# Summing modulation products over partitions: a transposing pass on VectorE and four matmuls per group of blocks, in place of four matmuls per block

## The reference, cut to what matters

```
def modulation(cond, w, b):
    m = jax.nn.silu(cond) @ w + b            # cond 1 x 1024, w 1024 x 9216, per layer and condition
    return m.reshape(cond.shape[0], 1, N_MOD, D_MODEL)
...
hp = hp + 0.5 * adaln_gate(m_ctx, 0) * swiglu(adaln_input(hp, m_ctx, 0, norm_g[i, 0]), ...)
hs = hs + 0.5 * adaln_gate(m_lat, 0) * swiglu(adaln_input(hs, m_lat, 0, norm_g[i, 0]), ...)
```

## Time and profile before

| | |
|---|---|
| device time, median of 3 runs | 1719.74 us (1719.39 to 1721.28) |
| profiled execution: span from first to last instruction | 1717.1 us |
| what lies around the span (median less span) | 2.6 us |
| TensorE busy | 1660.1 us, 97% of the span |
| VectorE busy | 1067.5 us, 62% |
| ScalarE busy | 578.3 us, 34% |
| mean granted TensorE clock | 0.976 of full speed |

### The profile page before, as it was taken

The page is one execution under the profiler, slowest core; times in us unless marked ns, Lnnn a source line. Parts: engine busy times, 40 slices in busy tenths (PEclk is TensorE's granted clock), DMA queues, the critical chain, the costliest instruction groups (busy, mean ns, idle before and its releaser), DMA issues.

```text
span 1717.1 us, 25878 instructions
## 1 busy us (share of the span) xinstructions
PE 1660.1 (97%) x9927; PEld 1589.1 (93%) x9927; DVE 1067.5 (62%) x1803; ACT 578.3 (34%) x751; POOL 81.3 (5%) x48
## 2 busy tenths in 40 slices
PE   8899999988899899999989999998999998999998
PEld 4899999988756899999989999998999998999998
DVE  3677668767754766767966777697745435334323
ACT  2423232253344442322234333222642325333222
POOL 1200000034100100000010000001000001000000
PEclk9999999989999899999989999999999998999999
DMA  9755547526200445555634545564533332433332
GB/s 310 187 182 164 192 159 244 170 85 207 77 1 31 157 146 173 177 189 196 224 120 135 193 161 195 190 226 157 186 124 96 125 123 85 136 122 122 124 130 77
DMA packets 222917, 261.81 MB, mean 152 GB/s; under 512 B 14502, under 2 KB 207494, under 8 KB 222854
## 3 DMA queue, kind: packets, MB, share of 16 engines
q1 hardware_dynamic: 222854, 260.95, 46.3%
HBM read 258.64 MB, written 2.29 MB: 152 GB/s over the span
## 4 chain that ended last, share of the span: by engine, by line
PE 86%; issue 6%; DVE 4%; ACT 1%; POOL 1%; DMA 0%; POOLq 0%; SPq 0%; ACTq 0%; DVEq 0%
PE ps L1066 15%; PE ps L1067 15%; PE ps L1069 15%; PE ps L1022 9%; PE ps L1024 9%; PE ps L1023 9%; PE ps L1055 3%; PE ps L1037 2%; PE ps L1257 1%; DVE macc L754 1%; PE ps L1126 1%; PE ps L1294 1%; POOL hrs L503 1%; PE ps L1363 1%; DVE w_lo L731 1%
## 5 line engine op out<-in xcount | busy, mean ns | idle before, releaser
L731 DVE TENSOR_TENSOR w_lo<-raw,w_hi 128x2048 fp32r<-128x2048 f32 x164 | 380.0, 2317 | 282.3 <-ACT w_hi L527 282.2
L1066 PE MATMUL ps<-x_hi,w_hi 128*128 128x384 f32 x1536 | 523.3, 341 | 13.2 <-ACT x_hi L553 9.9
L1067 PE MATMUL ps<-x_hi,w_lo 128*128 128x384 f32 x1536 | 520.1, 339 | 0.0
L1069 PE MATMUL ps<-x_lo,w_hi 128*128 128x384 f32 x1536 | 517.1, 338 | 0.0
L527 ACT ACTIVATE w_hi<-raw 128x2048 fp32r<-128x2048 f32 x169 | 322.9, 1911 | 344.2 <-PE ps L1024 326.3
L754 DVE SCALAR_TENSOR_TENSOR macc<-mraw,cT,macc 128x256 f32<-128x256 f32 x896 | 359.9, 478 | 0.0
L1066 PEld LDWEIGHTS ps<-x_hi,w_hi 128*128 128x128 f32 x1536 | 292.1, 190 | 17.0 <-issue 13.3
L1067 PEld LDWEIGHTS ps<-x_hi,w_lo 128*128 128x128 f32 x1536 | 292.1, 190 | 0.0
L1069 PEld LDWEIGHTS ps<-x_lo,w_hi 128*128 128x128 f32 x1536 | 291.3, 190 | 0.0
L1022 PE MATMUL ps<-act_hi,w_hi 128*128 (+1 forms) x832 | 281.8, 339 | 0.0
L1024 PE MATMUL ps<-act_hi,w_lo 128*128 (+1 forms) x832 | 279.6, 336 | 0.0
(11 more groups left out here) (154 smaller groups left out, 1310.7 us busy)
## 6 DMA issues: line engine op xcount, KB each, us to landing
raw<-ffn_w_gu SPq DMA_DIRECT2D x88, 1024.0 KB, 5.1
mraw<-mod_w SPq DMA_DIRECT2D x66, 1024.0 KB, 7.4
raw<-ffn_w_down SPq DMA_DIRECT2D x44, 1024.0 KB, 4.8
raw<-sgu_w_in SPq DMA_DIRECT2D x16, 1024.0 KB, 5.5
raw<-attn_w_in SPq DMA_DIRECT2D x9, 1024.0 KB, 5.0
raw<-sgu_w_out SPq DMA_DIRECT2D x8, 1024.0 KB, 4.8
mfirst<-mod_w SPq DMA_DIRECT2D x6, 1024.0 KB, 12.8
raw<-attn_w_out SPq DMA_DIRECT2D x4, 1024.0 KB, 4.9
```

Source lines behind the costliest of these rows:

```text
L731: nc.vector.tensor_tensor(w_lo[q0 % 2][:, :], raw[q0 % 2][:, :], w_hi[q0 % 2][:, :].bitcast(F32), ALU.subtract).then_inc(lo_done, 1)
L1066: mm(out, hi[:, cols], x_hi[:, k, :], start=(k == 0), stop=False)
L1067: mm(out, lo[:, cols], x_hi[:, k, :], start=False, stop=False)
L1069: last = mm(out, hi[:, cols], x_lo[:, k, :], start=False, stop=(k == KD - 1))
```

## The change

The sum over 128 partitions is split in two. Directly behind each block's `mod_sum`, VectorE runs one `tensor_reduce` with `apply_transpose` over the block's 128 x 512 sums: within each 32 x 32 square it transposes and then adds, so that each group of 32 partitions is summed, and 128 x 16 numbers go to a new tile `red` (room for 18 blocks). It waits for its own engine's last `mod_sum` instruction (`macc_done`). The rest, the sum over the four partition groups, is done by `mod_fold` on TensorE once per group of blocks, with four matmuls (32 columns of weights, `fold`; 4 columns per block moving). There are five groups and the lone first block: 18 blocks (feed-forward 0), 6 (projection and output projection), 18 (feed-forward 1), 18 (feed-forward 2) and 4 (stage V).

`mod_fold` of a group stands in a down stage, behind its last panel but one, and waits for all blocks of the group. `mod_out` is done once per group, behind VectorE's panel steps of that down stage, and TensorE waits for it inside the last panel, before the last bank. The `mod_psum` calls, their waits (`msum_done` in `mod_sum` and in `squares`, `mod_done` in `ffn`, in the attention's transposes and in `ready_ffn`) and the `mod_out` calls beside pairs, after `rotate()` and after the `wsn` products go away. TensorE's loop in `down` is two panels shorter, and these two stand behind it.

```diff
@@ mod_sum
-                if m >= 2:
-                    dve.wait_ge(msum_done, m + ii - 1)
...
                 last.then_inc(macc_done, 1)
+                dve.wait_ge(macc_done, m + ii + 1)
+                nc.vector.tensor_reduce(red[:, bass.ds(b0 - red_base(b0) + ii, 1), :].rearrange("p b n -> p (b n)"),
+                                        acc_of.rearrange("p c (n j) -> p (c n) j", j=32), AX.X, ALU.add,
+                                        apply_transpose=True).then_inc(red_done, 1)
@@ VectorE, ffn pair
-                    if b is not None:
-                        mod_out(b, ii, 1, ps[:, 6 + b % 2, 0:4], (msum_done, b + ii - MOD_SUM + 1))
@@ VectorE, down
                 steps_beside_blocks(dve, 0, blocks, n - 2, step)
+                if group is not None:
+                    mod_out(MOD_GROUPS[group][0], 0, MOD_GROUPS[group][1], ps[:, ORDER[-1], SPARE:SPARE + 4 * MOD_GROUPS[group][1]],
+                            (msum_done, group + 2))
                 gate(idx, j, w)
@@ TensorE
-            def mod_psum(b0, ii, bank, col, alone):
-                pe.wait_ge(macc_done, b0 + ii - MOD_SUM + 1)
-                for a in range(2):
-                    for cond in range(2):
-                        last = mm(ps[:, bank, bass.ds(col + 2 * a + cond, 1)], macc[:, b0 % 2, cond, P * a:P * a + P],
-                                  ones[:, 0:1], start=alone, stop=True, skip_group_check=not alone)
+            def mod_fold(b0, n, bank, col, alone):
+                pe.wait_ge(red_done, b0 + n - MOD_SUM)
+                for q in range(4):
+                    sums = red[:, 0:n, :].rearrange("p b (c a q) -> p b a c q", c=2, a=2)[:, :, :, :, q]
+                    last = mm(ps[32 * q:32 * q + 32, bank, col:col + 4 * n], fold[:, :], sums,
+                              start=alone, stop=True, skip_group_check=not alone)
                 last.then_inc(msum_done, 1)
@@ TensorE, ffn pair
-                    if b is not None:
-                        pe.wait_ge(mod_done, outs_until(b - 1) + ii)
-                        mod_psum(b, ii, 6 + b % 2, 0, True)
@@ TensorE, down
+                        if final and group is not None and m == ORDER[-1]:
+                            pe.wait_ge(mod_done, group + 2)
...
-                        if k == 3 and beside:
-                            mod_psum(block + j0 - 2, 2 * i, ORDER[-1], SPARE + 4 * (j0 - 2) + 8 * i, False)
...
+                    if fold_group is not None:
+                        mod_fold(*MOD_GROUPS[fold_group], ORDER[-1], SPARE, False)
...
-                steps_beside_blocks(pe, 2, min(blocks, n - 3), n - 1, panel)
-                panel(n - 1, 0, beside=blocks == n - 2, final=True)
+                its = (n - 4) // 2
+                if its:
+                    with pe.Fori(0, its) as i:
+                        panel(2, i)
+                        panel(3, i)
+                for j in range(2 + 2 * its, n - 1):
+                    panel(j, 0, fold_group=group if j == n - 2 else None)
+                panel(n - 1, 0, final=True)
@@ TensorE, attention transposes
-                    mod_psum(MOD_M + MOD_IN - 1, 0, 4, 4 * (MOD_IN - 1), True)
-                    pe.wait_ge(mod_done, outs_until(MOD_M + MOD_IN))
```

More of the change, by code:

```diff
@@ L86, in outs_until, with red_base @@
     return n
+def red_base(block):
+    return max([MOD_SUM] + [b for b, n in MOD_GROUPS if b <= block])
 def build(nc, t_in, t_out, toep_dram):
@@ L109, in build @@
             macc = sb("macc", [P, 2, 2, MB], scope=s)
+            red = sb("red", [P, MOD_GU + MOD_DN[0], 16], scope=s)
         sq = sb("sq", [P, 4, T])
@@ L115, in build @@
         mbT = sb("mbT", [P, DEPTH * NMOD * KD])
+        fold = sb("fold", [P, 32])
         ngT = sb("ngT", [P, DEPTH * 3 * KD])
@@ L527, in split, with squares @@
                 nc.scalar.activation(w_hi[q0 % 2][:, :], raw[q0 % 2][:, :], ACT.Copy).then_inc(hi_done, 1)
-            def squares(n, block=0):
+            def squares(n):
                 for k, m in enumerate(ORDER):
                     act.wait_ge(h_done, KD * n + k + 1)
-                    if k == 1 and block:
-                        act.wait_ge(msum_done, block - MOD_SUM)
                     if k >= 4:
@@ L662, in _ @@
             down(Q_OUT0, KD // 2)
-            squares(2, MOD_AT[1])
+            squares(2)
             split(Q_F[1] + 1, 0)
@@ L736, in mod_sum @@
                 m = b0 - MOD_SUM
+                acc_of = macc[:, b0 % 2, :, :]
                 if b0 == MOD_SUM:
@@ L838, in ffn, with down @@
                 loop_pairs(f, dve, pair)
-            def down(q0, n, idx, j, w, block=0, blocks=0):
+            def down(q0, n, idx, j, w, block=0, blocks=0, group=None):
                 def step(j0, i, beside):
@@ L855, in down @@
                         split(q0 + n, 0)
-                    if m == ORDER[-1] and blocks:
-                        mod_out(block, 0, blocks, ps[:, m, SPARE:SPARE + 4 * blocks],
-                                (msum_done, block + blocks - MOD_SUM))
+            dve.wait_ge(const_in, 16)
+            nc.vector.tensor_reduce(fold[:, :], ident[:, :].rearrange("p (g j) -> p j g", j=32), AX.X, ALU.add) \
+                .then_inc(fold_set, 1)
             dve.wait_ge(vecT_pe, 1)
@@ L962, in _ @@
             split(Q_OUT0 + 1, 0)
-            down(Q_OUT0, KD // 2, 1, (0, 1), 1.0, MOD_M + MOD_IN, MOD_OUT)
+            down(Q_OUT0, KD // 2, 1, (0, 1), 1.0, MOD_M + MOD_IN, MOD_OUT, 1)
             vectors(2, (0, 2))
@@ L967, in _ @@
             ffn(1)
-            down(Q_F[1] + 2 * GU, GU, 2, (0, 2), 0.5, MOD_AT[1] + MOD_GU, MOD_DN[1])
+            down(Q_F[1] + 2 * GU, GU, 2, (0, 2), 0.5, MOD_AT[1] + MOD_GU, MOD_DN[1], 2)
             vectors(3, (1, 0))
@@ L1007, in _ @@
                                         act_hi[:, 2 * g:2 * g + 2, :].bitcast(F32), ALU.subtract).then_inc(actl_done, 1)
-            down(Q_OUT1, KS // 2, 4, (1, 1), 1.0)
+            down(Q_OUT1, KS // 2, 4, (1, 1), 1.0, group=4)
             vectors(5, (1, 2))
@@ L1146, in pair, with down, panel @@
                     project(feature_major, q + 2 * g0 + 1, ii, 2)
-                    if b is not None:
-                        pe.wait_ge(mod_done, outs_until(b - 1) + ii)
-                        mod_psum(b, ii, 6 + b % 2, 0, True)
                 loop_pairs(f, pe, pair)
-            def down(q0, n, idx, hi, lo, ready, block=0, blocks=0):
-                def panel(j0, i, beside=False, first=False, final=False):
+            def down(q0, n, idx, hi, lo, ready, group=None):
+                def panel(j0, i, first=False, final=False, fold_group=None):
                     pe.wait_ge(lo_done, q0 + j0 + 2 * i + 1)
@@ L1224, in _ @@
             mod_rows(6)
-            mod_psum(MOD_SUM, 0, 2, 4 * MOD_SUM, True)
+            pe.wait_ge(fold_set, 1)
+            mod_fold(MOD_SUM, 1, 2, 4 * MOD_SUM, True)
             row_transposes(3)
             ffn(0, 0)
-            down(Q_F[0] + 2 * GU, GU, 0, act_hi, act_lo, ready_ffn(0), MOD_AT[0] + MOD_GU, MOD_DN[0])
+            down(Q_F[0] + 2 * GU, GU, 0, act_hi, act_lo, ready_ffn(0), 0)
             norm(1)
@@ L1381, in ready_sgu @@
                     pe.wait_ge(actl_done, UPAIR + 8)
-            down(Q_OUT1, KS // 2, 4, act_hi, act_lo, ready_sgu)
+            down(Q_OUT1, KS // 2, 4, act_hi, act_lo, ready_sgu, 4)
             norm(5)
```

29 lines of the change are left out of this document (11 added, 18 removed).

## The result

The changed kernel takes 1699.81 us (median of 4 runs, 1695.8 to 1703.28); the kernel before, beside it, 1719.57 (1717.19 to 1721.28). The ratio is 0.9878, 95% interval 0.9866 to 0.9890: about 20 us faster, where 34.9 were forecast. The time lies inside the stated range, 1676 to 1704, but outside the range of the forecast itself, 1677 to 1692.

What follows compares the result with a forecast made beforehand. TensorE was taken to bound the kernel, busy 97% of the span. The sum 25.2 + 16.4 + 2.1 - 0.9 - 2.5 - 1.7 - 3.7 = 34.9 us saved gave 1684.8 us, range 1676 to 1704.

Steps and rivals of the forecast that it cites:

- (a): Pairs: 30 blocks leave TensorE, 0.89 us saved in each of 29, the pass hidden in VectorE's room; net +25.2 us.
- (b): Three down stages: 7.2 us saved each, less 0.8 of TensorE waiting and 0.9 for the fold; net +16.4 us.
- (f): Clock: two longer TensorE waits, in the output projection and at 90 us, cost 1.8 us each; -3.7 us.
- (d): Output projection: TensorE idles 3.4 us for the pass before the last panel, then folds 0.9; net -2.5 us.
- (e): Projection: four passes in VectorE's chain lose 3.0 us, transposes no longer waiting for mod_out return 1.2; net -1.7 us.
- (c): Stage V: four sums leave TensorE, +3.6 us, less a 1.4 us wait for VectorE's split; net +2.1 us.
- X: Price of the pass on VectorE, per block: 0.74 us, lower bound 0.55, upper bound 2.3.
- Rivals 1 and 2: The pass is dearer: X 1.0 to 1.7, 1694 to 1718 us, 19%; or X 2.3, slower at 1744 us, 5%.
- the prediction's formula: Total saving in us: 58.4 - 32 X for X to 0.95, and 61 - 35 X beyond.
- Rival 3: Short waits in the three down stages and stage V also cost 1.8 us each: 7.3 more, 1692; 9%.
- (g): Nothing charged for the first block, fold itself, mod_out, SP's queue and the two unrolled panels.
- Rival 4: Something else sets the pair's or panel's pace, so (a) and (b) shrink; half gone is 21 us, 1706; 3%.

Runs made afterwards that it cites:

- the spare tile: Changed kernel plus an unused tile of 128 bytes a partition behind fold, so later tiles lie 256 bytes from their earlier place: 1691.59 us, ratio 0.9831.

## Why the prediction was right in direction and off in size

The stages can be told apart by GpSimd's `rs`, one per norm, with one more behind stage V. Before, and the changed kernel with the spare tile, so that no spacing blurs it:

```profile
353.03 1.77 POOL L486 TENSOR_TENSOR rs<-ms,mhalf 128x3 f32<-128x3 f32 x1 [3.71 <-DVE ms L791]
588.28 1.77 POOL L486 TENSOR_TENSOR rs<-ms,mhalf 128x3 f32<-128x3 f32 x1 [4.85 <-DVE ms L791]
893.20 1.77 POOL L486 TENSOR_TENSOR rs<-ms,mhalf 128x3 f32<-128x3 f32 x1 [4.97 <-DVE ms L791]
1196.34 1.77 POOL L486 TENSOR_TENSOR rs<-ms,mhalf 128x3 f32<-128x3 f32 x1 [3.71 <-DVE ms L791]
1282.41 0.85 POOL L512 TENSOR_TENSOR rs<-ms,mhalf 128x3 f32<-128x3 f32 x1 [84.30 <-DVE ms L984]
1425.18 1.77 POOL L486 TENSOR_TENSOR rs<-ms,mhalf 128x3 f32<-128x3 f32 x1 [3.70 <-DVE ms L791]
```

```profile
341.41 1.78 POOL L499 TENSOR_TENSOR rs<-ms,mhalf 128x3 f32<-128x3 f32 x1 [3.71 <-DVE ms L806]
588.60 1.77 POOL L499 TENSOR_TENSOR rs<-ms,mhalf 128x3 f32<-128x3 f32 x1 [4.00 <-DVE ms L806]
880.24 1.77 POOL L499 TENSOR_TENSOR rs<-ms,mhalf 128x3 f32<-128x3 f32 x1 [4.73 <-DVE ms L806]
1170.19 1.77 POOL L499 TENSOR_TENSOR rs<-ms,mhalf 128x3 f32<-128x3 f32 x1 [3.71 <-DVE ms L806]
1253.64 0.85 POOL L525 TENSOR_TENSOR rs<-ms,mhalf 128x3 f32<-128x3 f32 x1 [81.67 <-DVE ms L998]
1396.81 1.77 POOL L499 TENSOR_TENSOR rs<-ms,mhalf 128x3 f32<-128x3 f32 x1 [3.70 <-DVE ms L806]
```

| saved, us | forecast | measured (spare tile) | changed kernel |
|---|---|---|---|
| start and feed-forward 0: (a), (b), 1.8 of (f) | 11.0 | 11.6 | 10.2 |
| projection, attention, output projection: (d), (e), 1.8 of (f) | -6.0 | -11.9 | -13.7 |
| feed-forwards 1 and 2: (a), (b) | 28.8 | 26.5 | 29.3 |
| stage V: (c) | 2.1 | 2.6 | 1.9 |
| rest of the gated unit: the last fold | -0.9 | -0.4 | -1.3 |
| feed-forward 3 | 0 | 0.6 | -2.1 |
| sum | 34.9 (rounded terms) | 29.0 | 24.3 |

A single row is no better than 2 to 4 us: in its second profile the kernel before has 356.80 us for the first row, where it had 353.03, and 302.52 for feed-forward 1, where it had 304.92.

The down stages repeat far better. From the first matmul of one to its last, in feed-forward 1 of the changed kernel:

```profile
782.64 0.34 PE L1034 MATMUL ps<-act_hi,w_hi 128*128 128x384 f32 x1
...
876.62 0.34 PE L1036 MATMUL ps<-act_hi,w_lo 128*128 128x384 f32 x1
```

That is 93.98 us, and 94.0 in all three down stages with blocks, with the spare tile too; before it was 98.58, and without blocks, in feed-forward 3 before, it is 91.35.

- **The price of the pass** was right in kind and a little low. The nearest row, a plain reduction of the same kind, was the one to take: 0.71 us. But X, as VectorE's splits show it, was 0.84 in the down stages for the 0.74 of the sum; the wait for the own engine's last result, for which the prediction shows no row, was 0.15 and not 0.12, and little of the pass overlapped what follows. Rivals 1 and 2 fell. With X at 0.84 and, in the run with the pass twice, 9.58 - 8.27 = 1.31, the prediction's formula puts the second pass at 16.4 us; 18.2 were measured, so its slope was about right.
- **(a) Pairs**: right. 16.63 us a pair, and putting four matmuls back costs 0.89 us.
- **(b) Down stages**: the mechanism was right, the size was not. TensorE does wait in the last panels only, and the clock stays at 1.00 there. But with VectorE at 9.11 us a panel, and not 9.01, it waits before the last three panels, and the stage pays 93.98 - 91.35 = 2.6 us for waits and fold, where 0.8 and 0.9 were forecast. So each of the three stages gave 98.58 - 93.98 = 4.6 us and not 5.5, together 2.7 less. (The list of waits shows 0.8 a stage, the number of the forecast, but by luck: a matmul's record is 0.34 us long and the next can start 0.17 behind its start, so a wait costs more than the idle time that is listed.) Feed-forwards 1 and 2 together gave 29.3 us in one profile and 26.5 in the other, around the 28.8; this scatter lies outside the down stages and is not explained here.
- **(c), (d)**: right. In stage V short waits of under 0.6 us stand for the one of 1.4. The fold waits 3.4 us, the number that was forecast, the granted clock is 0.50 behind it (578 to 580 us), and a fold later in the last panel removes the wait.
- **(e) is the first step that failed**, the largest, and with it (f), which charged no clock there. "The transposes no longer wait for `mod_out`" was true, and the forecast booked 1.2 us for it as a gift. But they went ahead of a wait that stayed, `rope_done`. TensorE then idles 4.7 us, and behind the wait there is little in one piece, so the clock stays at half for some 20 us. Two different edits that remove this give 5.5 and 6.2 us back, nearly the whole 5.9 between -6.0 and -11.9. The rest of (e) was right: with the clock kept up, the output projection starts 196.8 us after the norm, against 195.3 before, 1.5 us later where the forecast had 1.7. Rival 3 named the clock, but looked for it in the down stages and stage V, whose waits of up to 0.6 us cost nothing of the kind.
- **(g) is the second**: "nothing" for `fold` itself. It costs no time as an instruction. But its 128 bytes moved all tiles behind it, and the large matmuls then ran at 174.7 or 176.7 ns in some stages: 1692.8 - 1688.1 = 4.7 us between the two profiles, 8 to 11 between the medians.
- **Rival 4** (TensorE isn't relieved) fell with the pairs' pace.
- **Luck.** With 5.9 and 4.7 the 34.9 become the 24.3 of the profile, but that nothing is left over is chance: the 2.7 us that the down stages gave less are made up by small gains elsewhere, 0.5 to 1.5 us each, within the scatter of a profile. And the stated range held the time only because it had been drawn up to 1704 for a dearer pass (rival 1), which didn't come; neither of the two failed steps is what it had been drawn for.

Open: why a shift of 128 bytes lets the spacing go and one of 256 doesn't, what picks one of the levels at the start of a stage, and whether other shifts are harmless; only 0, 128 and 256 were run. Why the shift costs the kernel before 17.9 us and the changed one 8 to 11 is also open; in before three feed-forwards landed on the slowest level at once, in one profile.

## What to carry to other kernels

A wait that is removed lets work run ahead, up to the next wait; look at what is then left behind that one, because here 4.7 us of idle time followed by small pieces on TensorE was paid with half the clock for some 20 us. A few unread matmuls in that place, or dense work kept behind the wait, won 6.2 and 5.5 us back. And a new tile is part of a change: when stages whose code is untouched get slower, count the matmuls in an equal window of both profiles, and try padding the allocation, as the 128 bytes here.

## What the runs showed of the hardware that was not expected

- The spacing of 384-column matmuls has three steady levels, 173.3, 174.7 and 176.7 ns, at a granted clock of 1.00. Which ones occur hangs on the place of the input tiles: 128 bytes of padding cost 17.9 us in one kernel and gained 8 to 11 in the other. The Trainium skill (SBUF — State Buffer, Operand start alignment) gives a rule of place, that an operand starts at a multiple of its element size, and adds: "This is about legality, not speed". All places here obey it, and the speed still differs.
- After 4.7 us without work the clock stayed at 0.50 for some 20 us while TensorE, in the second half of it, counted as 100% busy with small matmuls; after 6.06 us, with 30 transposes in one piece behind, it was whole again within 10 us. The Trainium skill (TensorE: Matmul & The Clock Gate, HAM oscillation) says that an idle gap makes the next piece start at the low clock; the trace agrees, and shows that what follows the gap sets how long this lasts.
- A `tensor_reduce` with `apply_transpose` takes 712 ns for 128 x 512 float32, 5% more than the 676 that a plain one would take by the two rows (an estimate), and 669 ns directly behind another one. Its price in VectorE's chain was 0.84 us a block in the down stages and 0.72 in stage V.
